# Reordering the first half of a two-block model kernel on one core: cross keys and values first, gate projections inside the attention heads, pairwise compression, fewer bias copies, taps in channel pairs

## The reference, cut to what matters

```
h = rms_norm(x, norm_mix_g)
u_conv, q, kc, vc, ks, vs, kw, vw, g_heads, g_conv, g_attn = split(h @ w_in)
# conv: v = a * sigmoid(gt); depthwise causal conv of width 31 over 1024 channels + bias;
#       layer norm, silu, then a 1024x1024 projection
# attention: 16 heads of 64, 4 key/value groups, three branches, each with its own softmax and a T5 bias:
#   compressed: blocks of 32 positions, stride 16 (15 blocks); z = block + pos;
#               sum over l of z[l] @ w1[l], silu, @ w2
#   selected and window: with 256 positions both see every earlier key
#   o = g0 * o_cmp + g1 * o_slc + g2 * o_win
x = x + (sigmoid(g_conv) * conv_out + sigmoid(g_attn) * o) @ w_out
h = rms_norm(x, norm_x_g)
k, v = split(mem @ xkv_w)            # depends on mem alone
x = x + softmax((h @ xq_w) k^T / 16) v @ xo_w
# then a SwiGLU, and the second block (gating, dilated attention, 128 experts)
```

## Time and profile before

| | us |
|---|---|
| median of three runs | 1870.79 (1870.45 to 1873.15) |
| the profiled execution, its own time | 1871.92 |
| its span, first to last instruction | 1870.1 |
| TensorE busy / weight load busy | 1712.6 / 1575.3 |
| VectorE / ScalarE / GpSimd busy | 1243.7 / 799.3 / 151.6 |
| mean granted TensorE clock | 0.933 of full |
| first product of a weight unit | starts at 28.5 |
| 69 units and the compression | 28.5 to 276 |
| the 16 heads | 276 to 395 |
| conv tail up to the first pw product | 395 to 419.5 |
| pw, wout, cross attention, SwiGLU, second block | 419.5 to 1870.1 |

### The profile page before, as it was taken

How to read it: one execution, slowest core, us unless ns; L and a number is a source line. 1 busy time by engine, 2 the same in 40 slices (tenths; PEclk the granted TensorE clock), 3 DMA queues, 4 the chain that set the end, 5 groups by cost and what they waited for, 6 DMA issues and landing times.

```text
span 1870.1 us, 33160 instructions
## 1 busy us (share of the span) xinstructions
PE 1712.6 (92%) x11502; PEld 1575.3 (84%) x11502; DVE 1243.7 (67%) x2364; ACT 799.3 (43%) x1334; POOL 151.6 (8%) x287
## 2 busy tenths in 40 slices
PE   5899998869989999887799999599999999999997
PEld 4899986549879999775799999599999888888885
DVE  4499494445536665562579978766666888886665
ACT  3344244433435444443446666333333333335443
POOL 4000103300000000000000000011111111110000
PEclk8999797879989999895799999799999999999998
DMA  9955350004426555340235555344444444446663
GB/s 208 243 177 167 119 199 2 1 1 137 133 79 204 180 180 188 103 155 3 91 105 171 186 180 180 101 135 141 139 137 143 135 145 140 142 145 191 193 195 105
DMA packets 71638, 260.90 MB, mean 140 GB/s; under 512 B 8256, under 2 KB 8384, under 8 KB 71312
## 3 DMA queue, kind: packets, MB, share of 16 engines
q1 hardware_dynamic: 67536, 245.92, 40.7%
q0 software_dynamic: 4032, 14.04, 3.5%
HBM read 254.68 MB, written 5.24 MB: 139 GB/s over the span
## 4 chain that ended last, share of the span: by engine, by line
PE 74%; issue 11%; DVE 9%; ACT 3%; DMA 2%; POOL 1%; DVEq 0%; POOLq 0%; ACTq 0%; SPq 0%
PE bank L328 15%; PE bank L329 15%; PE bank L330 15%; PE bank L748 6%; PE bank L769 3%; PE bank L771 3%; PE bank L770 3%; DVE ring_lo L1231 2%; DVE arena L1317 1%; DMA ring_raw<-in_stream 1%; PE bank L363 1%; PE bank L364 1%; PE bank L365 1%; PE bank L429 1%; PE bank L379 1%
## 5 line engine op out<-in xcount | busy, mean ns | idle before, releaser
L1231 DVE TENSOR_TENSOR ring_lo<-ring_raw,ring_hi 128x1024 fp32r<-128x1024 f32 x467 | 594.6, 1277 | 194.5 <-ACT ring_hi L874 187.5
L328 PE MATMUL bank<-operand_hi,ring_hi 128*128 128x256 f32 x2272 | 660.4, 291 | 38.3 <-DVE operand_lo L1273 27.7
L329 PE MATMUL bank<-operand_lo,ring_hi 128*128 128x256 f32 x2272 | 651.6, 287 | 0.0
L330 PE MATMUL bank<-operand_hi,ring_lo 128*128 128x256 f32 x2272 | 651.4, 287 | 0.0
L874 ACT ACTIVATE ring_hi<-ring_raw 128x1024 fp32r<-128x1024 f32 x467 | 490.0, 1050 | 122.3 <-PE bank L330 47.4
L328 PEld LDWEIGHTS bank<-operand_hi,ring_hi 128*128 128x128 f32 x2272 | 445.5, 196 | 41.8 <-DVE operand_lo L1273 27.9
L329 PEld LDWEIGHTS bank<-operand_lo,ring_hi 128*128 128x128 f32 x2272 | 445.2, 196 | 0.1
L330 PEld LDWEIGHTS bank<-operand_hi,ring_lo 128*128 128x128 f32 x2272 | 444.5, 196 | 0.0
L769 PE MATMUL bank<-ring_hi,hidden_hi 128*128 128x512 f32 x512 | 206.1, 402 | 0.0
L771 PE MATMUL bank<-ring_hi,hidden_lo 128*128 128x512 f32 x512 | 200.5, 392 | 0.0
L770 PE MATMUL bank<-ring_lo,hidden_hi 128*128 128x512 f32 x512 | 199.2, 389 | 0.0
(11 more groups left out here) (253 smaller groups left out, 1857.9 us busy)
## 6 DMA issues: line engine op xcount, KB each, us to landing
ring_raw<-in_stream SPq DMA_DIRECT2D x467, 512.0 KB, 3.5
bias_rows<-arena POOLq DMA_DIRECT2D x1, 4096.0 KB, 48.7
arena<-bias_rows POOLq DMA_DIRECT2D x16, 192.0 KB, 4.1
arena<-in_w POOLq DMA_DIRECT2D x4, 512.0 KB, 11.8
arena<-in_xT POOLq DMA_DIRECT2D x1, 1024.0 KB, 8.2
arena<-in_memT POOLq DMA_DIRECT2D x1, 1024.0 KB, 6.0
out_rows<-arena SPq DMA_DIRECT2D x2, 512.0 KB, 2.7
arena<-in_wsT POOLq DMA_DIRECT2D x1, 512.0 KB, 3.5
```

The source lines that it names most:

```text
L328: pe.matmul(out, wh, xh, start=start, stop=False, **kw)
L329: pe.matmul(out, wh, xl, start=False, stop=False, **kw)
L330: return pe.matmul(out, wl, xh, start=False, stop=stop, **kw)
L1231: dve.tensor_tensor(w_lo[:, slot, :], raw[:, slot, :], w_hi[:, slot, :].bitcast(F32), ALU.subtract)\
```

## The change

- **Cross keys and values first.** The stream begins with xk and xv; mem is loaded first, and O_MEM becomes the first operand. The norm of x runs on TensorE between xk and xv. Then come kc, vc, uconv, q, ks, kw. x is squared on ScalarE.
- **Gate projections inside the heads.** The units gates (1) and v (4) run between the first scores and the first transposes; gattn and gconv (16 units) run one behind each head's value products, into bank 5. Their sigmoid is taken once for all at the end (two instructions of 128 x 2048), and the product with the attention output becomes one instruction of 128 x 2048. Both evacuations of transposed probabilities, and that of the compressed ones, go to ScalarE.
- **Compression by two positions a product.** Partitions 0 to 63 of z hold one key position and 64 to 127 the next; z is filled by eight DMAs from SBUF to SBUF (64 partitions each), pos is a fifth group of columns. TensorE does 16 products of 75 columns for keys and 16 for values, with contiguous `w1`.
- **Fewer bias copies.** The bias rows are written 16 times rather than 128 (0.5 MB rather than 4 MB), and the skewed table is loaded by eight DMAs, each of 16 partitions and all heads (8 x 384 KB, 3 MB as before).
- **Taps in channel pairs**, from an explicit counter: three behind each unit from the fifth uconv unit to the last kw unit, then 10 up to the loop over heads, six in each head, and the rest behind the last head.

```diff
+SHIFTS = 16
-STAGES = [("uconv", 16), ("q", 8), ("kc", 2), ("vc", 2), ("ks", 2), ("kw", 2), ("v", 4), ("gates", 1),
-          ("gconv", 8), ("gattn", 8), ("xk", 8), ("xv", 8), ("pw", 8), ("wout", 8), ("xq", 8), ("xo", 8),
+STAGES = [("xk", 8), ("xv", 8), ("kc", 2), ("vc", 2), ("uconv", 16), ("q", 8), ("ks", 2), ("kw", 2), ("gates", 1), ("v", 4),
+          ("gattn", 8), ("gconv", 8), ("pw", 8), ("wout", 8), ("xq", 8), ("xo", 8),
...
-                for l in range(CMP_BLOCK):
-                    m = pe.matmul(bank[kv][:, 0:2 * NCMP], w1[kv][:, l, :], z[kv][:, l, :, :].rearrange("p a b -> p (a b)"),
-                                  start=l == 0, stop=l == CMP_BLOCK - 1)
+                for l in range(CMP_BLOCK // 2):
+                    m = pe.matmul(bank[kv][0:HD, 0:(G + 1) * NCMP], w1[:, kv, l, :],
+                                  z[kv][:, :, 2 * l:2 * l + CMP_STRIDE * (NCMP - 1) + 1:CMP_STRIDE],
+                                  start=l == 0, stop=l == CMP_BLOCK // 2 - 1)
...
             for hh in range(NH):
                 if hh + 2 < NH:
                     nsa_scores(hh + 2)
                 if hh + 1 < NH:
                     nsa_transposes(hh + 1)
                 nsa_values(hh)
+                project_cols(U["gattn"] + hh, 5, ("gate", hh))
...
-            pool.dma_start(bias_d.ap(), brow[0:NH].unsqueeze(1).to_broadcast([NH, P, 512])).then_inc(brow_out, 16)
+            pool.dma_start(bias_d.ap(), brow[0:NH].unsqueeze(1).to_broadcast([NH, SHIFTS, 512])).then_inc(brow_out, 16)
...
+            for p0 in range(0, P, SHIFTS):
+                rows = bass.AP(bias_d, P - 1 - p0, [[511, SHIFTS], [SHIFTS * 512, NH], [1, 384]])
+                pool.dma_start(bias[p0:p0 + SHIFTS, :, :], rows).then_inc(bias_in, 16)
...
             def tap(n):
-                k, c = n // KC, n % KC
+                pair, k, c = n // (2 * CONV_W), n // 2 % CONV_W, n % 2
+                c += 2 * pair
...
-                    dve.wait_ge(taps, n - KC + 1)
+                    dve.wait_ge(taps, n - 1)
...
             for hh in range(NH):
...
                 if hh + 2 < NH:
                     nsa_bias(hh + 2)
-                if s == 0 and hh:
-                    nsa_gated(hh // 2 - 1)
-            nsa_gated(KC - 1)
+                if hh and hh % 2 == 0:
+                    nsa_out(hh // 2 - 1)
+                lo_to(U["gattn"] + hh + RING)
+                some_taps(2)
+                if hh + 2 < NH:
+                    nsa_scale(hh + 2)
+                some_taps(4)
+            some_taps(KC * CONV_W)
+            nsa_out(KC - 1)
```

More of the change, by code:

```diff
@@ L264, in build @@
         U = FIRST
-        (O_MIX, O_MEM, O_CONV, O_Y, O_X, O_XO, O_FFN, O_2, O_MIX2, O_PEER, O_EXP) = range(11)
-        FIRST_USE = [U[n] for n in ("uconv", "xk", "pw", "wout", "xq", "xo", "ffn", "ua", "wout2", "wq2", "expert_u")]
+        (O_MEM, O_MIX, O_CONV, O_Y, O_X, O_XO, O_FFN, O_2, O_MIX2, O_PEER, O_EXP) = range(11)
+        FIRST_USE = [U[n] for n in ("xk", "kc", "pw", "wout", "xq", "xo", "ffn", "ua", "wout2", "wq2", "expert_u")]
         FROM_PSUM = (O_XO, O_MIX2)
@@ L390, in norm_cols @@
                 m.then_inc(col_sum, 1)
+            cj = 0
+            for n in range(8):
+                project_cols(U["xk"] + n, 4 + cj % 4, ("xk", n), O_MEM if n == 0 else None)
+                cj += 1
             pe.wait_ge(onehot_in, 32)
@@ L483, in nsa_values @@
                 if s == 0:
-                    take(4 + c % 2, ("o", c))
-                o = bank[4 + c % 2]
+                    take(4, ("o", c))
+                o = bank[4]
                 for name in (("pT", 0, hh), ("pT", 1, hh), ("sc", hh)):
@@ L496, in _ @@
             nsa_scores(0)
+            u = U["gates"]
+            unit(u)
+            for t in range(TT):
+                t0 = slice(t * P, (t + 1) * P)
+                take(4 + t, ("gates", t))
+                for c in range(KC):
+                    n0 = slice(c * P, c * P + 3 * NH)
+                    o, s = bank[4 + t][:, 0:3 * NH], u % RING
+                    pe.matmul(o, a_hi[:, c, t0], w_hi[:, s, n0], start=c == 0, stop=False)
+                    pe.matmul(o, a_hi[:, c, t0], w_lo[:, s, n0], start=False, stop=False)
+                    m = pe.matmul(o, a_lo[:, c, t0], w_hi[:, s, n0], start=False, stop=c == KC - 1)
+            m.then_inc(unit_done, 1)
             nsa_scores(1)
+            project_rows(U["v"], 2, "v")
             nsa_transposes(0)
+            drained(4, 5)
             for hh in range(NH):
@@ L937, in row_std @@
                 act.activation(v, v, ACT.Sqrt, bias=eps[:, 0:1]).then_inc(stat_std, 1)
-            hi_to(RING)
+            operand(O_MEM, lambda c: hf[:, c, :], lambda c: act.wait_ge(mem_in, 16))
+            act.wait_ge(x_in, 16)
+            act.activation(sq, xT, ACT.Square).then_inc(norm_sq, 1)
+            for j in range(8):
+                copy_cols("xk", j, kx[:, j, :])
             act.wait_ge(brow_done, 1)
@@ L943, in _ @@
             norm(N_MIX)
+            for half in range(2):
+                copy_rows(f"xv{half}", U["xv"] + 4 * half, [vx[:, t, half * 512:(half + 1) * 512] for t in range(TT)])
             act.wait_ge(consts_in, 48)
             normed_operand(O_MIX, 0)
+            for name, dst in (("kc", kcT), ("vc", vcT)):
+                for j in range(2):
+                    copy_cols(name, j, dst[:, j, :])
             for j in range(KC):
@@ L975, in _ @@
                .then_inc(bank_free[3], 1)
-            operand(O_MEM, lambda c: hf[:, c, :], lambda c: act.wait_ge(mem_in, 16))
-            for j in range(8):
-                copy_cols("xk", j, kx[:, j, :])
-            for half in range(2):
-                copy_rows(f"xv{half}", U["xv"] + 4 * half, [vx[:, t, half * 512:(half + 1) * 512] for t in range(TT)])
             def nsa_exp(hh):
@@ L1295, in _, with glu @@
             dve.scalar_tensor_tensor(mean2[:, :, 1], cols[:, G_FINAL, :], 1.0 / D, cols[:, G_FINAL, :], ALU.mult, ALU.mult)
+            lo_to(U["xv"] + RING)
+            normed(N_MIX, G_MIX, hf)
+            operand_rest(O_MIX, lambda c: hf[:, c, :])
             dve.wait_ge(init, 3)
-            for j in range(KC):
-                from_unit(U["uconv"] + 2 * j + 1)
+            dve.wait_ge(brow_out, 16)
+            def glu(j):
+                dve.wait_ge(unit_done, U["uconv"] + 2 * j + 2)
                 emptied(dve, ("uconv", 2 * j + 1))
```

210 lines of the change are left out of this document (100 added, 110 removed).

## The result

| | before | forecast | measured |
|---|---|---|---|
| median of the runs, us | 1870.79 (1870.45 to 1874.18, 7 runs) | 1852 (1826 to 1870) | 1877.66 (1875.01 to 1880.93, 7 runs) |
| profiled execution, its span | 1871.92, 1870.1 | | 1877.55, 1875.8 |

The changed kernel takes 1.0035 times as long as the kernel before, 95% interval 1.0025 to 1.0045: slower, by more than 0.2%. The forecast was wrong in sign, and the time lies outside its range.

The account below looks back on a forecast made before the run. It took TensorE and VectorE near their limits in dense stretches, then heads, compression and slow start as bounds. Summed positions put the first pw product at 400.8, 18.7 us earlier: 1871.9 became 1853.2, less 1.1 gives 1852 (1826 to 1870).

Parts of the forecast that it names:

- Start: From the kernel's start, with no norm ahead of the products: first product at 12.7 us, bounds 12 and 15.
- keys and values: Keys and values of mem, with x's norm between them and the operand replaced after: done at 66.9 us.
- kc to kw: The 32 units after mem's keys and values: 2.84 us each, 90.9 in all, VectorE not a limit.
- Transfers: Under kc to kw, the table load onto 16 partitions leaves weights short: 14 us, between 0 and 20, reaching 171.8.
- Compression: Compression of keys and values in 64 half products: 6.4 to 13 us, taken as 7.5.
- Heads: Loop over heads: period 8.6 us, TensorE's 7.8 plus 0.8 from taps blocking GpSimd's scaling; ends at 339.2.
- no blocking: Rival in the heads: taps and GpSimd don't block each other, period 7.8, 11 us less, 1841; chance 0.15.
- 0.7 to spare: In the heads, the other engines' 7.0 us from bias work to scaling fits into 9.6 with 0.7 us left.
- Tail of taps: Behind the last head: 76 taps at 0.396 us take 30.1 us while TensorE waits; ends at 372.0.
- Layer norm: After the last taps: 24.4 us as before, 3.0 for low clock, 1.4 for low operand; first pw product 400.8.
- the one on the other side: Rival in the heads: clock falls for every second head's attention part, period 10.2, 23 us more, 1875; chance 0.11.

Follow-up runs that it names:

- the kicked kernel: The kernel before, with GpSimd's second and fourth multiply of the first expert down loop made to wait until VectorE's `lo` is done: 1872.68 us (0.9999).
- the run with the wide table: The changed kernel with `lo` made to wait for GpSimd's multiply and the bias table loaded a head a DMA onto 128 partitions: 1843.21 us (0.9836).

## Why the prediction was wrong

The step that failed is the first sentence of the sum: "Everything from the first pw product (419.5 us) on keeps its order, so I build the new time of that product." It takes for granted that what keeps its order keeps its time. That part kept its order, began 22.0 us earlier and ended 5.7 later in the profiled executions: 22.5 us went in the down loop and 6.0 in the cross attention, and 0.8 came back elsewhere. The runs put in its place: in that loop GpSimd beats `lo` to SBUF by 0.06 us, a margin that I had before me and used only as evidence that two instructions block each other. The change issues three GpSimd instructions fewer ahead of the loop, GpSimd's first answer of an iteration comes 0.09 us later, and the order flips in every second block. The place of the loop alone does it: minus three in the kernel before makes the loop 21.6 us longer, plus one or plus three in the changed kernel make it 230.0 us again. The second part is 6.0 us of a lower granted clock in the cross attention; it is in the profiled execution of every version of the change (29.2 to 29.6 us) but the one with the moved taps alone, it is in none of the kernel before (23.2 to 23.3 in five), and no run isolates its cause.

The rest, by the prediction's own steps:
- *Start* 12.7, *keys and values* 66.9, *kc to kw*: 12.55 and 65.91; right within a microsecond.
- *Transfers*, 14 us between 0 and 20: kc to the compression took 104.9 where dense units take 90.9, so 14.0. Eight pieces took a median of 21.4 us each to land. In other runs of the same code the compression came up to 5 us later, so this term varies by itself, and that it came out at 14.0 is partly luck. The shape of the pieces, 16 partitions each, is the cause, as taken: on 128 partitions the compression begins 13.6 us earlier.
- *Compression* 7.5, bounds 6.4 and 13: 8.45.
- *Heads*, 8.6: a pair takes 16.97, so 8.5 on average, and one head took 10.9 at a granted clock of 0.91. The number is right by luck, for the reason is another. GpSimd's six instructions are stretched as foreseen (mean 505 ns; 2.84 to 3.00 us for six instead of 2.18), yet TensorE doesn't wait for them: it waited 1.0 us in every second head for the copy out of the bank that the change leaves the pairs to share (bank 4 in place of banks 4 and 5). The diff shows that; I priced GpSimd instead. With the copy moved, the period is 7.96 with the scaling stretched as much, so the blocking cost nothing and the rival "no blocking" had the right period. The prediction's "0.7 to spare" also does not follow from its terms: 9.6 less 7.0 is 2.6, and it is 0.6 only if the `lo` and the two taps that now stand between, 2.0 us, are taken off, which the text does not say.
- *Tail of taps*, end 372.0: 371.51.
- *Layer norm* up to the first pw product: 26.0, forecast 28.8. The sums took 5.28 and 5.40 us where 6.6 for each was forecast (3.67 and 6.63 before), which is 2.5 of the 2.8 us.
- Of the rivals, the one on the other side blamed the clock in the heads; there it stayed at 0.91 to 1.00 (200 to 340 us, stretches of 20). The clock did take 6 us, in the cross attention. No rival named the loop.

## What to carry to other kernels

A saving of time at the front reaches the end only if every later loop keeps its rhythm; look there for two instructions of different engines that start within 0.1 us of each other and block each other, and treat that order as luck. One wait that fixes the order costs nothing where the loser has slack, and here it is worth 22 us. Work that is taken from under a busy engine must be put under idle time elsewhere, or it returns at the end: the 76 taps cost 27.5 us behind the heads, and 1.1 us (heads of 121.8 instead of 120.7) once they were put into the 22 us in which VectorE idled and into the heads themselves.

## What the runs showed of the hardware

GpSimd's answer to a semaphore in a loop depends on where the loop stands among its instructions: 0.19 us, or 0.28 for the first wait of every iteration when the loop begins at place 213 (0.51 to 0.52 at its entry). Code written out straight answered in 0.08 us (the two unkicked blocks of the kicked kernel). What sits at that place stays open. The Trainium skill (Runtime: NRT & Kernel Launch, Instruction fetch mechanics) says that instructions are fetched in blocks of 256 and that a branch to a block that is not held waits for a fetch. An edge right behind place 213 fits the loops begun at 213 and 214; but the trace shows one or two instruction packets in the whole loop in either kernel, not one for each of 32 iterations, and in the run with the wide table the loop over the early blocks (places 210 to 218) lies across the same place and answers in 0.19.

The shape of a DMA's target decides how much bandwidth other queues are left with: with the same DMA engines full and the table moving equally fast, 275 GB/s in all against 188.
